# A one-core transformer block pair in float32: memory rows loaded and scaled one stage earlier, the output stage's vector order turned round, the vectors' transposition moved up

## What is computed

```python
u = rms_norm(x, norm_mix_g);  proj = u @ w_in
conv_out = silu(layer_norm(depthwise_conv(...))) @ w_conv_out
mla_out  = causal_attention(...) @ w_mla_out
h = x + (gate0 * conv_out + gate1 * mla_out) @ w_out
u = rms_norm(h, norm_xattn_g)
mem_n = rms_norm(mem, norm_mem_g)                  # mem: 256 rows x 1024
h = h + softmax(q(u) @ k(mem_n).T) @ v(mem_n) @ w_xo
u = rms_norm(h, norm_mlp_g)
h = h + square(relu(u @ w_mlp1)) @ w_mlp2
```

## Time and profile before

| | |
|---|---|
| median of 3 runs | 1414.56 us (1413.9 to 1415.56) |
| the profiled execution's own time | 1414.13 us |
| its span, first to last instruction | 1412.3 us |
| PE busy | 1383.6 us, 98% of the span, 6429 matmuls |
| DVE busy | 787.9 us, 56% |
| ACT busy | 599.2 us, 42% |
| POOL busy | 74.3 us, 5% |
| HBM traffic | 89 GB/s over the span |
| mean granted PE clock | 0.995 |

### The profile page before, as it was taken

How to read it: one execution, slowest core, us unless ns; L and a number is a source line. 1 busy time by engine, 2 the same in 40 slices (tenths; PEclk the granted TensorE clock), 3 DMA queues, 4 the chain that set the end, 5 groups by cost and what they waited for, 6 DMA issues and landing times.

```text
span 1412.3 us, 19005 instructions
## 1 busy us (share of the span) xinstructions
PE 1383.6 (98%) x6429; PEld 1110.9 (79%) x6429; DVE 787.9 (56%) x1250; ACT 599.2 (42%) x1010; POOL 74.3 (5%) x60
## 2 busy tenths in 40 slices
PE   7999999997999999999999999999999999999998
PEld 5787777776886888888888888778778778778886
DVE  6438888875466543335445575454464464465553
ACT  5535655545354443214333365343344344333233
POOL 1000000101103000000013300000000000000000
PEclk9999999998999999999999999999999999999999
DMA  5323323223422333333332332323323323323322
GB/s 156 90 69 79 71 57 96 75 84 95 121 88 76 92 102 104 89 89 105 89 104 89 92 102 86 90 71 93 91 62 93 93 60 93 93 60 104 101 99 84
DMA packets 228143, 126.67 MB, mean 90 GB/s; under 512 B 17107, under 2 KB 220964, under 8 KB 228099
## 3 DMA queue, kind: packets, MB, share of 16 engines
q1 hardware_dynamic: 226482, 123.47, 30.2%
q10 hardware_dynamic: 1616, 2.62, 0.5%
HBM read 123.98 MB, written 2.10 MB: 89 GB/s over the span
## 4 chain that ended last, share of the span: by engine, by line
PE 92%; DVE 3%; ACT 2%; issue 1%; DMA 1%; ACTq 0%; DVEq 0%; SPq 0%
PE lin L606 26%; PE lin L610 25%; PE lin L609 25%; PE ob L721 2%; PE sc L685 1%; PE sc L708 1%; PE tr L697 1%; DVE wl L1561 1%; ACT wh L1128 1%; DMA xtok<-in_x_dram 1%; PE tr L1031 1%; PE tr L650 0%; PE tr L708 0%; PE ob L697 0%; DMA raw<-in_w_out_dram 0%
## 5 line engine op out<-in xcount | busy, mean ns | idle before, releaser
L1561 DVE TENSOR_TENSOR wl<-raw,wh 128x1024 fp32r<-128x1024 f32 x238 | 288.6, 1220 | 190.0 <-ACT wh L1128 185.1
L1128 ACT ACTIVATE wh<-raw 128x1024 fp32r<-128x1024 f32 x238 | 239.6, 1012 | 124.0 <-DMA raw<-in_w_mlp_dram 45.3
L606 PE MATMUL lin<-uh,wh 128*128 128x512 f32 x624 | 253.4, 406 | 4.0 <-DVE ul L1611 1.4
L610 PE MATMUL lin<-uh,wl 128*128 128x512 f32 x624 | 244.1, 391 | 0.0
L609 PE MATMUL lin<-ul,wh 128*128 128x512 f32 x624 | 243.9, 391 | 0.0
L606 PE MATMUL lin<-vh,wh 128*128 128x512 f32 x576 | 232.2, 403 | 0.0
L610 PE MATMUL lin<-vh,wl 128*128 128x512 f32 x576 | 225.4, 391 | 0.0
L609 PE MATMUL lin<-vl,wh 128*128 128x512 f32 x576 | 224.3, 389 | 0.0
L606 PEld LDWEIGHTS lin<-uh,wh 128*128 128x128 f32 x624 | 117.8, 189 | 32.9 <-issue 4.1
L609 PEld LDWEIGHTS lin<-ul,wh 128*128 128x128 f32 x624 | 117.9, 189 | 25.0 <-issue 2.6
L610 PEld LDWEIGHTS lin<-uh,wl 128*128 128x128 f32 x624 | 117.5, 188 | 25.3
(11 more groups left out here) (478 smaller groups left out, 1886.9 us busy)
## 6 DMA issues: line engine op xcount, KB each, us to landing
raw<-in_w_in_dram SPq DMA_DIRECT2D x100, 512.0 KB, 3.8
raw<-in_w_mlp_dram SPq DMA_DIRECT2D x64, 512.0 KB, 4.0
raw<-in_w_out_dram SPq DMA_DIRECT2D x16, 512.0 KB, 3.6
raw<-in_w_xkv_dram SPq DMA_DIRECT2D x8, 512.0 KB, 3.5
raw<-in_w_proj_b_dram SPq DMA_DIRECT2D x8, 512.0 KB, 3.5
raw<-in_w_proj_a_dram SPq DMA_DIRECT2D x8, 512.0 KB, 3.6
xtok<-in_x_dram ACTq DMA_DIRECT2D x4, 512.0 KB, 5.3
raw<-in_w_mla_out_dram SPq DMA_DIRECT2D x4, 512.0 KB, 3.3
```

The lines of the kernel that those rows point to most:

```text
L606: ins = pe.matmul(o, wh[:, slot, at], xh_, start=start, stop=False)
L610: return pe.matmul(o, wl[:, slot, at], xh_, start=False, stop=stop)
L1128: act.activation(wh[:, c.slot(4), 0:size], raw[:, c.slot(2), 0:size], ACT.Copy).then_inc(hi_made, 1)
L1561: dve.tensor_tensor(wl[:, c.slot(4), 0:size], raw[:, c.slot(2), 0:size], wh[:, c.slot(4), 0:size].bitcast(F32), ALU.subtract).then_inc(lo_ ...
```

## The change

There are four edits.

1. `memtok` now lies over the upper half of `xul` (tiles 4 to 7 of the cross attention's low input), and `xul` begins below it. SP loads it ahead of the last of the four conv_out chunks, and waits for `y_tanh`, the last reader of what lay there.
2. The squares, the sum and the Sqrt of the memory rows stand on ACT at the end of step m == 1 of the conv_out stage. DVE's reciprocal stands at the end of its step m == 2, and the scaling is now two ACT instructions at the end of ACT's step m == 2, in place of two DVE instructions in w_out.
3. `MEM_TURNS` places the eight turns in jobs 0 to 2 of w_out, where they stood in jobs 2 to 4.
4. In the xo stage DVE adds tile f to `h` before it makes the low part of tile f - 1. The chunk's lowering stands behind the addition.

A fifth is small: at the start, PE turns `vrows` before the fourth tile of `xn`, where it stood behind it.

```diff
-MEM_TURNS = {2: {4: 0, 5: 1, 6: 2}, 3: {1: 3, 3: 4, 5: 5, 7: 6}, 4: {1: 7}}
+MEM_TURNS = {0: {2: 0, 4: 1, 6: 2}, 1: {1: 3, 4: 4, 7: 5}, 2: {2: 6, 5: 7}}
...
         xuh = sb("xuh", [P, DT, S], F32R, st)
-        xul = sb("xul", [P, DT, S], F32R, st)
         s2 = ExitStack()
+        s2.enter_context(nc.sbuf_tensor("low_xul", [P, DT // 2, S], F32))
         memtok = sb("memtok", [P, 2, D], stack=s2)
         s2.close()
+        xul = sb("xul", [P, DT, S], F32R, st)
...
             stream("mla_out", a["w_mla_out"][0], 0, 4, 256)
-            stream("conv_out", a["w_conv_out"][0], 0, 4, 256)
+            c, _ = phase("conv_out")
+            for m in range(4):
+                if m == 3:
+
+                    sp.wait_ge(y_tanh, CT)
+                    sp.dma_start(memtok[:], a["mem"][0].rearrange("(q p) n -> p q n", p=P)).then_inc(mem_landed, 16)
+                load(c + m, a["w_conv_out"][0], 256 * m, 4, 256)
...
             for m, (kind, n) in enumerate(W_ORDER):
-                if m == 2:
-
-                    sp.wait_ge(m_made, DT)
-                    sp.dma_start(memtok[:], a["mem"][0].rearrange("(q p) n -> p q n", p=P)).then_inc(mem_landed, 16)
                 load(c + m, a["w_out"][0] if kind == "w" else a["w_xkv"][0], P * n, DT, P)
...
             for q in range(QT):
+                if q == QT - 1:
+                    pe.wait_ge(vecs_landed, 16 * len(VECS))
+                    pe.transpose(tr[0][:, 0:NVEC], vrows[0:NVEC, :], ident[0:NVEC, 0:NVEC]).then_inc(vec_ready, 1)
                 pe.wait_ge(x_landed[q], 16)
                 pe.wait_ge(xn_made, q + 1)
                 for f in range(DT - 2):
                     ins = turn_normed(q, f)
                     if q == QT - 1:
                         ins.then_inc(xt_ready, 1)
-            pe.wait_ge(vecs_landed, 16 * len(VECS))
-            pe.transpose(tr[0][:, 0:NVEC], vrows[0:NVEC, :], ident[0:NVEC, 0:NVEC]).then_inc(vec_ready, 1)
             turn_late(DT - 2)
...
                 if m == 1:
                     act.wait_ge(mem_landed, 16)
...
                     act.activation(std[:, 0:2], mem_sq, ACT.Sqrt, bias=eps, scale=1.0 / D).then_inc(std_made, 1)
+                if m == 2:
+                    act.wait_ge(rstd_made, NORM_NO["mem"] + 1)
+                    for q in range(2):
+                        act.activation(memtok[:, q, :], memtok[:, q, :], ACT.Copy, scale=mem_rstd[:, q:q + 1])\
+                            .then_inc(mem_scaled, 1)
...
                 lower(c + (m + 2))
                 for f in (2 * m, 2 * m + 1):
                     merge(f, j + f, gates, gates[:, DT:2 * DT, :], 0)
+                if m == 2:
+                    dve.wait_ge(std_made, NORM_NO["mem"] + 1)
+                    dve.reciprocal(mem_rstd, std[:, 0:2]).then_inc(rstd_made, 1)
...
-                if m == 2:
-                    dve.wait_ge(std_made, NORM_NO["mem"] + 1)
-                    dve.reciprocal(mem_rstd, std[:, 0:2]).then_inc(rstd_made, 1)
-                    dve.wait_ge(rstd_made, NORM_NO["mem"] + 1)
-                    dve.wait_ge(mem_landed, 16)
-                    for q in range(2):
-                        dve.tensor_scalar(memtok[:, q, :], memtok[:, q, :], mem_rstd[:, q:q + 1], None, ALU.mult)\
-                            .then_inc(mem_scaled, 1)
...
             c, j = phase("xo")
-            for m in range(4):
-                lower(c + (m + 2))
-                for f in (2 * m, 2 * m + 1):
-                    add_to_h(f, j + f)
-                    evacuated(dve, j + f)
-                    gain_low(ul[:, f, :], h[:, f, :], col("norm_mlp_g", f), uh[:, f, :], U0["mlp"] + f + 1)
+
+            def mlp_low(f):
+                evacuated(dve, j + f)
+                gain_low(ul[:, f, :], h[:, f, :], col("norm_mlp_g", f), uh[:, f, :], U0["mlp"] + f + 1)
+
+            for f in range(DT):
+                add_to_h(f, j + f)
+                if f % 2 == 0:
+                    lower(c + (f // 2 + 2))
+                if f:
+                    mlp_low(f - 1)
+            mlp_low(DT - 1)
```

More of the change, by code:

```diff
@@ L1293, in _ @@
                     act.activation(uh[:, f, :], (tc, td)[f % 2][:], ACT.Copy).then_inc(m_high, 1)
-            c, j = phase("w_out")
-            for m, (kind, n) in enumerate(W_ORDER):
-                split(c + (m + 2))
-                if m and W_ORDER[m - 1][0] == "w":
-                    f = W_ORDER[m - 1][1]
-                    evacuated(act, j + (m - 1))
-                    gain_high(xuh[:, f, :], h[:, f, :], col("norm_xattn_g", f))
-                    square("xattn", f, h[:, f, :])
                 if m == 1:
@@ L1312, in _ @@
                     act.activation(std[:, 0:2], mem_sq, ACT.Sqrt, bias=eps, scale=1.0 / D).then_inc(std_made, 1)
+                if m == 2:
[3 more added lines that the diff above has]
+                            .then_inc(mem_scaled, 1)
+            c, j = phase("w_out")
+            for m, (kind, n) in enumerate(W_ORDER):
+                split(c + (m + 2))
+                if m and W_ORDER[m - 1][0] == "w":
+                    f = W_ORDER[m - 1][1]
+                    evacuated(act, j + (m - 1))
+                    gain_high(xuh[:, f, :], h[:, f, :], col("norm_xattn_g", f))
+                    square("xattn", f, h[:, f, :])
                 for f in MEM_TURNS.get(m, {}).values():
```

## The result

| | before | after |
|---|---|---|
| median of 4 runs each | 1414.99 us (1413.9 to 1415.56) | 1405.82 us (1405.29 to 1405.97) |
| profiled execution, own time | 1414.13 us | 1405.74 us |
| its span | 1412.3 us | 1403.9 us |
| mean granted PE clock | 0.995 | 0.998 |

The ratio is 0.9934 with a 95% interval of 0.9922 to 0.9947: the change makes the kernel 0.66% faster. The forecast was 1405.3.

A forecast was written before the change was run, and what follows sets the result against it. PE, 92% of the chain, was taken as the bound, so only its waits and slow work could pay. Gains of 1.15 + 5.6 + 2.2 = 8.95 us gave 1405.3; likeliest 1404 to 1407 (0.62), 1401.5 to 1408.5 some 0.8.

The forecast's parts named there:

- Start: Before the first product: turning vrows earlier lets cols be copied near 12.2 instead of 13.35, gaining 1.15 us.
- Work put into conv_out: In conv_out: ACT's added memory work delays splits DVE waits for, losing 3.84 and 2.09 us.
- the rival in which this work is hidden: conv_out: ACT has room, so the 5.93 us are not lost, 1399.3; half hidden 1402; chance 0.12 for both.
- The table load: ACT in conv_out: the skill's 2.66 us per switch, against 1.28 in the trace, would make the time 1406.6.
- The clock: conv_out: PE's clock may halve in the new 4.3 us gap; the slow job costs at most 0.1 us.
- the second delay: conv_out: ACT's scalings make the next split 2.09 us later still, which hides the slow job.
- the old gap: w_out before the change: PE stood 7.30 us up to 332.51, then ran at 0.5 clock for about 5 us.
- w_out: w_out: rows scaled before the stage and no load waiting for m_made gain 11.7 us.
- xo: xo stage: additions no longer stand behind low parts waiting for ACT, so PE sets the pace; 2.2 us gained.
- a longer low clock: End of conv_out into w_out: half clock for one or two more jobs, 1408.0 or 1410.7; chance 0.12.
- no gain in xo or at the start: xo bound by ACT gives 1407.5, or late gain vectors at the start 1406.5; chance 0.10 together.
- slower than before: w_out: low clock holds throughout, 1417 us and more; low clock through w_out 0.04, slower 0.03.

The follow-up runs named there:

- The gaps version: Changed kernel with ACT's memory work moved behind the splits of conv_out steps 1, 2 and 3; 1399.3 us, and 1400.24 us when timed again.
- the old turns: Changed kernel with the eight turns put back in jobs 2 to 4 of w_out; 1405.81 us.
- the lowering first: Changed kernel with the xo lowering put back ahead of the even tile's addition, additions still ahead of the low parts; 1407.23 us.
- The early load alone: Kernel before with only memtok's new place and its load in conv_out; squares, Sqrt and scaling stay in w_out; 1407.56 us.
- start-only: Kernel before with only vrows turned ahead of the fourth tile; 1412.33 us.
- xo-only: Kernel before with only the xo stage's new vector order; 1412.0 us.
- the squares behind the split: Changed kernel with only squares, table load and Sqrt moved behind the split of m == 2, scalings left in place; 1402.77 us.

## Why the prediction was right

- **Start.** Forecast `cols` near 12.2, first product near 14.5, 1.15 us gained; measured 12.23, 14.54 and 1.12. The path was right, the match to the hundredth was luck. The forecast kept the fourth tile's scaling at 11.49 and let `cols` follow it at once. The scaling began at 11.03, since the input rows landed earlier, and `cols` then waited 0.44 us more for PE, which turned `vrows` at 11.85, behind the third tile. The two errors cancel.
- **Work put into conv_out.** Forecast 3.84 + 2.09 = 5.93 lost, a wait of 4.3, w_out's first job near 314.7; measured 6.06, a wait of 4.25, and 314.75. The split came 3.84 us late as summed (300.80 - 1.18 + 3.84 = 303.46, measured 303.44). The scalings took 2.10 up to the split, where the prediction took 1.9 to 2.0. The gaps version turns the argument round: same work, other place, no loss. So the rival in which this work is hidden fell for the kernel as written, and its price (1399.3) is the time of the version that does hide it.
- **The table load.** The Trainium skill's larger figure for a switch ("ScalarE: Activation LUTs", "What ACT_TABLE_LOAD costs") was weighed and left. Load, Sqrt and the start of the split took 1.28 and 1.50 us (301.94 to 303.44), as before; the trace shows no drain beside them.
- **The clock.** Forecast: it falls in the new gap, the slow job is hidden by the second delay, and it comes back after some 5 us of work. It fell, and it was hidden. It came back after 3.3 us of work here, after 3.9 with the old turns and 6.0 with the lowering first. The 5 us of the forecast, taken from the old gap, were too long; that the size didn't matter is shown by the 93.19 us of two executions with such different stretches.
- **w_out.** Forecast 11.7 gained, with conv_out 5.8 net, 5.6 taken; measured 11.44 and 5.38. The early load alone moves the landmark by 8.3 us net of the start. The prediction tied the gain to rows scaled before the stage; it didn't see that most of it comes from the load alone. The 11.4 also hang on one execution of the kernel before: behind the old wait PE worked at the low clock for 5.5 us there (to 338.0), for 4.7 and 3.1 us in the start-only and the xo-only kernel, and w_out took 74.84 us, against 74.60 and 73.97.
- **xo.** Forecast 2.2, jobs 2.7 us apart; measured 2.41, jobs 2.72 apart. The addition ahead of the low part makes 1.04 us of it, the lowering behind the addition 1.37.
- **The sum.** 8.95 forecast, 9.12 at the last matmul, 8.39 in the profiled executions' own times (0.7 us go in the tail, which the forecast left out), 9.17 between the medians. The rivals with a longer low clock, no gain in xo or at the start, and slower than before have no row that speaks for them. The one execution with 6.8 us of low clock lost nothing by it.

## What to carry to other kernels

On an engine that works in order, what an added instruction costs is not its duration but where it stands. Ahead of an instruction for which another engine waits, it costs all of its time (6 us here). In the gaps behind, where its own engine waits, it costs nothing, up to about the sum of the gaps until the next thing waited for (2.6 and 1.3 us here). So find the engine's waits first, by the idle time ahead of its rows, and put the work into these, not simply where its data are ready. When a load and the work on it move together, try each place of the work with the same load. Up to the first `tr<-ones,logit` the load alone gained 8.3 us, with the work ahead of the splits 5.4, and with the work in the gaps 11.5.

## What the runs showed of the hardware that was not expected

**The clock can fall after the wait is over.** With the squares behind the split PE stood 2.58 us up to 310.82, and the granted clock fell only at about 312.3, with PE busy all the time, and was back at about 315.7. With the old turns it fell about half a microsecond after PE had resumed, with 4.25 us of standing before. In the changed kernel it fell just before PE resumed. The same wait of 4.2 us came with a low stretch of 3.4 us in three kernels and of 6.8 in a fourth, and the old wait of 7.3 us with 10.2 us in one and 6.8 in two.

**The first products scatter.** The gaps version was profiled twice. In one the first conv_out product came at 284.94 and the own time was 1399.63; in the other at 286.12 and 1400.84. So 1.18 of 1.21 us arise before conv_out, 0.20 of them before the first product. The second one's first products:

```profile
14.74 0.76 PE L609 MATMUL lin<-uh,wh 128*128 128x512 f32 x1 [0.16 <-DVE ul L1621]
15.30 0.63 PE L612 MATMUL lin<-ul,wh 128*128 128x512 f32 x1
15.73 0.63 PE L613 MATMUL lin<-uh,wl 128*128 128x512 f32 x1
```

They begin 0.43 to 0.56 us apart. In the first profile they begin 0.23 to 0.31 apart, each later one 0.39 long. The granted clock is shown as 1.00 from 15 to 17 us in both profiles, so here the column didn't show what the durations did. Three of the thirteen profiles have such a start: this one, the xo kernel with the lowering first, and xo only, where the column does show it (0.50 from 17 to 19 us). From the first product to conv_out's first it takes 271.4, 271.4 and 272.0 us in them, and 270.4 to 270.5 in the other ten. So it costs 1 to 1.6 us, as much as the start's whole gain.

It doesn't explain why the start-only and the xo-only kernel measured more than their mechanisms. The start-only profile has no slow start, and its excess of 0.69 us lies before the first product. The xo-only profile has one, and yet its own time (1411.94) is that of its median. What remains is that three stretches which a change leaves alone (the landing of the input rows, the first products, the clock behind a long wait) each move by up to 1 us or more from one execution to the next. How they mix in the medians is open, as one execution of each kernel has a trace, and two of the gaps version.
